# Two transformer blocks on one core: five plain pairs in place of six, seventeen groups of block products in place of sixteen, and low halves made by an accumulating DMA

## The reference, cut to what matters

```python
def first_block(x, ...):
    h = rmsnorm(x, ln1[l]);  z = h @ w_in[l]
    ...                                          # three mixers, then w_o
    h = rmsnorm(x, ln2[l])
    gate, up = jnp.split(h @ w_gu[l], 2, axis=-1)          # 2 x 2816 columns
    x = x + (jax.nn.silu(gate) * up) @ w_down[l]
    return rmsnorm(x, ln_f)

def second_block(x, ...):                        # projections, two attentions, merge
    ...
```

## Time and profile before

| | us |
|---|---|
| runs | 1033.74, 1036.65, 1036.48 (median 1036.48) |
| profiled execution, its own time | 1035.21 |
| its span, first to last instruction | 1033.4 |
| TensorE busy | 1014.9 (98%) |
| VectorE, ScalarE, GpSimd busy | 680.8, 500.8, 334.1 |
| granted TensorE clock, mean | 0.998 |

### The profile page before, as it was taken

How to read it: one execution, slowest core, us unless ns; L and a number is a source line. 1 busy time by engine, 2 the same in 40 slices (tenths; PEclk the granted TensorE clock), 3 DMA queues, 4 the chain that set the end, 5 groups by cost and what they waited for, 6 DMA issues and landing times.

```text
span 1033.4 us, 15311 instructions
## 1 busy us (share of the span) xinstructions
PE 1014.9 (98%) x5694; PEld 847.1 (82%) x5694; DVE 680.8 (66%) x1264; ACT 500.8 (48%) x928; POOL 334.1 (32%) x396
## 2 busy tenths in 40 slices
PE   9999999999999999999999999999999999999996
PEld 7887877788789999999998778767887777788885
DVE  6875657578757677677677657799756766235553
ACT  6433656554544444444445647446754555233233
POOL 1354632441121111011103657333436756421101
PEclk9999999999999999999999999999999999999999
DMA  8312233123254454454442736211223332223212
GB/s 296 103 62 82 83 95 92 62 65 105 101 139 120 104 142 98 118 136 112 110 102 79 221 107 202 81 62 62 82 82 93 97 113 87 103 84 100 102 62 81
DMA packets 42536, 109.29 MB, mean 106 GB/s; under 512 B 5456, under 2 KB 8976, under 8 KB 42464
## 3 DMA queue, kind: packets, MB, share of 16 engines
q1 hardware_dynamic: 36720, 96.80, 28.9%
q0 software_dynamic: 5328, 11.01, 6.4%
q10 hardware_dynamic: 416, 0.52, 0.2%
HBM read 100.22 MB, written 4.74 MB: 102 GB/s over the span
## 4 chain that ended last, share of the span: by engine, by line
PE 62%; DVE 5%; ACT 2%; DMA 2%; issue 1%; DVEq 0%; ACTq 0%
PE bank L1774 13%; PE bank L1775 12%; PE bank L1776 12%; PE bank L1788 5%; PE bank L1790 5%; PE bank L1789 5%; PE bank L1938 2%; PE bank L1929 1%; DVE score L2619 1%; DVE m L2617 1%; PE bank L1914 1%; DMA WL<-wall 1%; PE bank L1822 1%; PE bank L1824 1%; PE bank L1823 1%
## 5 line engine op out<-in xcount | busy, mean ns | idle before, releaser
L2714 POOL TENSOR_TENSOR WL<-WS,WH 128x256 fp32r<-128x256 f32 x256 | 203.1, 794 | 250.6 <-ACT WH L1992 234.6
L1774 PE MATMUL bank<-HH,WH 128*128 128x512 f32 x600 | 243.9, 406 | 2.6 <-DVE fa L2556 2.2
L1776 PE MATMUL bank<-HH,WL 128*128 128x512 f32 x600 | 234.6, 391 | 0.0
L1775 PE MATMUL bank<-HL,WH 128*128 128x512 f32 x600 | 234.3, 391 | 0.0
L1774 PEld LDWEIGHTS bank<-HH,WH 128*128 128x128 f32 x600 | 113.2, 189 | 30.7 <-issue 3.8
L1992 ACT ACTIVATE WH<-WS 128x1024 fp32r<-128x1024 f32 (+1 forms) x130 | 133.2, 1034 | 2.9 <-DMA WS<-wall 2.8
L1776 PEld LDWEIGHTS bank<-HH,WL 128*128 128x128 f32 x600 | 112.6, 188 | 24.5
L1775 PEld LDWEIGHTS bank<-HL,WH 128*128 128x128 f32 x600 | 113.1, 188 | 20.8 <-issue 1.2
L2481 DVE TENSOR_TENSOR WL<-SS,WH 128x512 fp32r<-128x512 f32 x112 | 76.0, 692 | 46.5 <-ACT WH L2136 46.2
L2136 ACT ACTIVATE WH<-SS 128x512 fp32r<-128x512 f32 x112 | 66.6, 623 | 75.0 <-DVE SS L2478 57.1
L2756 POOL DMA_DIRECT2D SS<-wall x32 | 27.8, 867 | 213.9 <-DVE SS L2478 140.5
(11 more groups left out here) (374 smaller groups left out, 2264.3 us busy)
## 6 DMA issues: line engine op xcount, KB each, us to landing
WS<-wall SPq DMA_DIRECT2D x129, 512.0 KB, 3.5
SS<-wall SPq DMA_DIRECT2D x48, 256.0 KB, 3.5
SS<-wall POOLq DMA_DIRECT2D x32, 256.0 KB, 4.1
WL<-wall POOLq DMA_DIRECT2D x5, 512.0 KB, 8.2
scratch<-rows SPq DMA_DIRECT2D x8, 320.0 KB, 5.8
b_t<-scratch SPq DMA_DIRECT2D x8, 256.0 KB, 3.4
X<-xT SPq DMA_DIRECT2D x7, 256.0 KB, 6.0
outT<-X SPq DMA_DIRECT2D x7, 256.0 KB, 2.4
```

Source lines behind the costliest of these rows:

```text
L1774: e.matmul(b[:, :], wh, xh, start=k == 0, stop=False)
L1775: e.matmul(b[:, :], wh, xl, start=False, stop=False)
L1776: m = e.matmul(b[:, :], wl, xh, start=False, stop=k == n - 1)
L2714: e.tensor_tensor(WLS[:, at_c:at_c + 256], WS[:, u % NST, cs], f32(WHS[:, at_c:at_c + 256]), ALU.subtract).then_inc(*tick(w_low_g, u if c ...
```

## The change

Pair 5 becomes a group of block products, so five plain pairs stand in front and seventeen groups follow. While the plain pairs run, the units' low halves are made in the "dma" way with look 3. The steps of `halves_normed` are placed by another `SIDE`. The first unit of down (group 6) is split at position 5 of its period in place of 2. Behind the last group, the "dma" way starts two steps of down earlier, and the products of gains and the table load (`gain_product`, `load_ln`) come behind one more split. `slot()` notes the user of both places of a wrapping unit. Since 17 x 7 blocks are an odd number of places, units behind the groups wrap where they did not before.

```diff
-OLD_PAIRS = 6
+OLD_PAIRS = 5
 CHUNKS = (0, 6, 10, 16, 22)
-WITH_UNIT = tuple(range(15))
+WITH_UNIT = tuple(range(1, 16))
...
-            before = slots["user"][at_s:at_s + n]
-            slots["user"][at_s:at_s + n] = [user] * n
+            at = [(at_s + i) % (2 * NW) for i in range(n)]
+            before = [slots["user"][i] for i in at]
+            for i in at:
+                slots["user"][i] = user
...
-        SIDE = set(range(42, 34, -1)) | set(range(34, 12, -2))
+        SIDE = {n for n in range(11, 35) if n > 26 or n % 4}
...
                 nh = halves_normed()
+                now["low"], now["look"] = "dma", 3
...
-        now["low"] = w_low_v
+        now["low"], now["look"] = w_low_v, 2
...
-                if at == 2 or at == 4 and g == NPAIR - 1:
+                if g in unit_of and at == (5 if g == 6 else 2) or g == NPAIR - 1 and at in (2, 4):
                     split()
...
-        do("gain_product")
-        do("load_ln")
...
-        for _ in range(6):
+        for _ in range(4):
             next(downs)
         split()
         assert not line_up, line_up
+        do("gain_product")
+        do("load_ln")
         now["low"], now["look"] = "dma", 3
```

## The result

Seventeen runs of each kernel, taken together: 1037.97 us (1035.93 to 1039.61) against 1035.12 us (1033.67 to 1036.65) before. The ratio is 1.0026, with a 95% interval of 1.0019 to 1.0033. The forecast was 2.98 us less; it became 2.85 us more. (The three runs that the forecast of 1033.5 us starts from have a median 1.36 us above that of the seventeen.)

The account below looks back on a forecast made before the run. It took TensorE, busy 98% of the span, and its feed-forward waits as the bound; -0.80 - 2.46 - 1.52 + 2.5 - 0.7 = -2.98 us took the runs' median of 1036.48 to 1033.5 us, range 1030.3 to 1037.6.

Parts of the forecast that it names:

- Pair 5's form: Pair 5 loses 48 matmuls of 512 columns and gains 84 of 256: -0.80 us.
- The first group: TensorE's wait on VectorE's `WL` at the first group's second product goes: -1.52 us.
- The rival of late blocks: First group: block T3's DMA lands after 7.6 us in place of 4.1, +2.9 us, 1036.4 us; chance 0.14.
- Where down starts: Down's first product newly waits for pair 5's low half of `GA`, at its sixth tile: +2.5 us.
- The plain pairs: `WL` rows leave the chain from gate to silu, so waits on `fa` shrink, 0.6 of 3.06 left: -2.46 us.
- the rival that GpSimd's multiply sets `fa`: Plain pairs: the multiply, not VectorE's `WL`, sets `fa`, so -2.46 becomes 0: 1036.0 us; chance 0.10.
- The tail: Behind down, the wait on the DMA goes, half the gain given back for the last column's just-in-time `HL`: -0.7 us.
- The low halves by DMA: Plain pairs: six units' rows of -high on ScalarE and DMA issues on GpSimd, landings in time: counted 0.
- The rival of late landings: Plain pairs: low halves land late, five units by 1 to 2 us each, +7.0 us, 1043.5 us; chance 0.12.

Follow-up runs that it names:

- The split at 2: The changed kernel with down's first unit split at position 2 in place of 5: 1035.73 us, ratio 1.0006 to the kernel before.
- the interleaving: The changed kernel with the first two products of down's first chunk interleaved: 1034.29 us, ratio 0.9990 to the kernel before.
- The empty place: The interleaved kernel with one ring place left empty ahead of the tail's units, so none behind the groups wraps: 1033.11 us, ratio 0.9980.
- the old tail: The changed kernel with only the tail of down as in the kernel before: 1036.90 us, ratio 1.0023 to the kernel before.
- the second trace: The profiled execution of the unaltered changed kernel when measured once more, beside the kernel before: 1038.51 us over six runs, ratio 1.0031.

## Why the prediction was wrong

The bound (TensorE, and the waits of the feed-forward part) was read rightly, and so were three terms of five. Taking the steps in turn:

- **Pair 5's form, -0.80.** The middle of the program is the same to 0.01 us, and the two groups ahead of down take 18.84 for 13 products of 12 matmuls, 18.72 by the pitch. Right.
- **The first group, -1.52.** The wait on `WL` is gone; 0.12 is left. Right. The rival of late blocks did not happen in the changed kernel. Waits in the first group came up as soon as the plain pairs were made shorter; whether late blocks made them is not shown.
- **Where down starts, +2.5.** 2.57. Right, mechanism and size: from the tanh (start 300.62) to the end of the low half (309.73) it is 9.11 us against 6.79 in the earlier trace rows, 2.32 more, where I had 2.37. The split at 2 and the interleaving confirm it from two sides.
- **The plain pairs, -2.46.** This step failed. From 250.26 six products should end at 282.90, and the groups start at 285.09: 2.19 lost where I left 0.6, so -0.87. The sum took a `WL` out of the way from gate to silu and put nothing for the steps of `halves_normed` that stand there and between silu and `fa` now. They "no longer have a `WH` ahead of them", but they have ScalarE's own row ahead instead, of the same length, and one of them was stretched beside GpSimd's multiply. ScalarE, GpSimd and VectorE of the changed kernel at the third pair; the last line shows the first of the two `n_s` by itself:

```profile
261.12 1.06 ACT L2000 ACTIVATE WL<-WH 128x1024 fp32r<-128x1024 f32 x1
262.09 2.94 ACT L2152 ACTIVATE n_s<-NF 128x1024 fp32r<-128x1024 f32 x3
...
262.48 0.86 POOL L2710 DMA_DIRECT2D WL<-wall  x1 [8.52 <-ACT WL L2000]
263.05 1.63 POOL L2764 TENSOR_TENSOR fg<-fg,Rb 128x512 f32<-128x512 f32 x1
...
260.18 1.23 DVE L2539 SCALAR_TENSOR_TENSOR n_A<-NF,n_A 128x1024 fp32r<-128x1024 f32 x1 [1.65 <-ACT n_A L2152]
261.32 0.69 DVE L2553 SCALAR_TENSOR_TENSOR fg<-fs,fg 128x512 f32<-128x512 f32 x1
263.16 3.74 DVE L2539 SCALAR_TENSOR_TENSOR n_s<-NF,n_s 128x1024 fp32r<-128x1024 f32 x2 [1.16 <-ACT n_s L2152]
266.82 0.68 DVE L2559 TENSOR_TENSOR fa<-bank,fg 128x512 f32<-128x512 f32 x1
...
263.16 2.60 DVE L2539 SCALAR_TENSOR_TENSOR n_s<-NF,n_s 128x1024 fp32r<-128x1024 f32 x1 [1.16 <-ACT n_s L2152]
```

The silu waits behind an `n_A` that waited 1.65 us for ScalarE. Even so GpSimd's product is done at 264.68, some 2 us sooner than before. But `fa` stands behind two `n_s` until 266.82, and TensorE's up starts at 267.56, where it started at 267.57 before. The first `n_s` waits 1.16 us for ScalarE, where the row of -high, which I had counted at nothing, stands just ahead of its copy. Then it takes 2.60 us, where the other three `n_s` of this trace take 1.21 or 1.22: it starts while GpSimd's multiply runs and ends 1.08 us after it. Without these 1.38 us `fa` would start at 265.44 (an estimate) and be done before TensorE comes to the wait at 266.75, so the wait of 0.81 would be gone.

The Trainium skill's rule (SBUF — State Buffer, "Who interferes with whom") is borne out by this. The prediction saw nothing in rows 5 that proves it, and had it stretch the multiply; in the changed kernel it stretched VectorE's step. The trace before has the reverse at the same pair, where the multiply starts in a running `n_A`, ends 1.16 us after it, and takes 2.15 us, where one with no such row beside it takes 1.29:

```profile
264.36 1.22 DVE L2536 SCALAR_TENSOR_TENSOR n_A<-NF,n_A 128x1024 fp32r<-128x1024 f32 x1
...
264.59 2.15 POOL L2761 TENSOR_TENSOR fg<-fg,Rb 128x512 f32<-128x512 f32 x1 [11.04 <-DVE fg L2550]
```

The long `n_s` (2.58 to 2.60 us) is there in all six traces with the changed kernel's `SIDE` and the dma way. Where the steps were moved, no such row of VectorE runs beside the third pair's multiply, all `n_s` take 1.22, and both waits are gone. So it is shown that these rows of VectorE made the waits. The experiment moved the rows and the overlap together, so how much of the wait is the 1.38 us is read from the rows alone.

At the fourth pair it is the silu that gains nothing, and there `fa` does follow the multiply:

```profile
276.10 0.68 DVE L2553 SCALAR_TENSOR_TENSOR fg<-fs,fg 128x512 f32<-128x512 f32 x1
...
277.05 1.61 POOL L2764 TENSOR_TENSOR fg<-fg,Rb 128x512 f32<-128x512 f32 x1
...
278.75 0.69 DVE L2559 TENSOR_TENSOR fa<-bank,fg 128x512 f32<-128x512 f32 x1 [1.96 <-PE bank L1779]
```

The silu starts at 276.10, at 276.05 before: an `n_A` ahead of it waits 1.65 us for ScalarE, as long as the `WL` before did for its `WH`. The multiply ends at 278.66 and `fa` starts at 278.75. (Its row puts the wait down to TensorE, but the product that it reads began at 267.56 and was over at about 273.) What is gained (279.50 against 279.84) is the multiply's time, 1.61 against 2.13 us. So the rival that GpSimd's multiply sets `fa` is refuted for the third pair and true of the last step at the fourth.

- **The tail, -0.7.** This failed too: +0.97. The wait on the DMA went, as said, but TensorE met the columns that GpSimd paces, and these had become slower by the wrapped unit's second issue. For the units that wrap the sum had only rows of ScalarE and VectorE, at nothing; GpSimd's issue of 0.88 was not among them. I had the 0.88 as the upper end and then took half of a gain. The row to go by was the one that said "just in time": a chain without slack gets nothing from an earlier TensorE and pays every addition. The empty place shows it, the old tail shows that the move itself is neutral.
- **The low halves by DMA, 0.** Right for the landings: no wait on them, 8.8 us at most. The rival of late landings did not happen. The row of -high was not free, as said above.
- **What was not in the sum at all.** The clock. I priced the wait at down with the time it lasts, and had no rival for what comes behind it. In most executions it costs another 1.5 us: seen in the second trace, told for the others by the clock that they list, and gone with the wait.

By terms: -2.98, +1.6 for the plain pairs, +1.7 for the tail, +0.4 in small parts (0.3 of it behind the last matmul, not explained) gives the +0.7 of the trace. With the clock's 1.5 it is 2.2 of the 2.85 between the medians. The other 0.6 is open; the changed kernel's first trace is also its fastest run, and the ten traces differ by up to 1.4 us in the stretch ahead of the plain stage alone.

The Trainium skill (TensorE: Matmul & The Clock Gate, "What's actually happening") says that the gate's watch runs freely and doesn't start with the kernel. That would let the same wait be followed by a fall in one execution and not in another, and the two traces of the changed kernel show that much; that this is the reason is not shown.

## What to carry to other kernels

Price a new wait on TensorE at more than its length: here 2.3 us of waiting were followed in the second trace by 3.4 us at 1.2 GHz, most executions list a lower clock, and removing the wait gave 4.2 us. When rows leave an engine's list, look what each row that moves up waits for itself; a two-engine step waits on its partner as the old one did, and here one that met GpSimd's multiply took 2.60 us in place of 1.22. And before a gain is booked ahead of a stage that is just in time, find what paces that stage and count what the change adds to it, here one DMA issue of 0.88 us from an odd number of places in a ring.

## What the runs showed of the hardware

The fall of the clock came a good microsecond after TensorE had started again (310.14 to about 311.5), not in the wait itself. It followed waits of 2.27 us (in one trace of two) and 1.91 us, and did not follow waits of 2.72 and 2.28 us in the trace that has the 1.91. With the longest wait at 0.73 us or less in that place, all 22 runs of the two kernels (first two products interleaved, split at 2) list 0.997 or 0.998.

In these traces a step of VectorE with two inputs in SBUF and GpSimd's multiply did not run side by side. The one that started second took longer: 2.60 us in place of 1.22 for VectorE, 2.15 in place of 1.29 for GpSimd, and ended about 1.1 us after the other.
